# Experts of a mixture-of-experts stage taken in the order of their token counts, found on the chip

## The reference, cut to what matters

```
logits = xt @ w_router + b_router                      # 256 x 32
top_logits, top_idx = top_k(logits, 4); top_w = softmax(top_logits)
for each expert e, for its tokens:
    gate, up = split(xb @ w_gu[e] + b_gu[e], 2)
    act = (clip(up, -7, 7) + 1) * (min(gate, 7) * sigmoid(1.702 * gate))
    y[tok] += top_w * (act @ w_dn[e] + b_dn[e])
```

## Time and profile before

| | |
|---|---|
| median of 3 runs | 2322.34 us |
| lowest, highest | 2320.06, 2329.26 us |
| the profiled execution | 2318.49 us, span 2316.6 us |
| granted TensorE clock over the span | 0.983 |
| busy TensorE, VectorE, ScalarE | 2165.1, 751.5, 468.7 us |
| share of q1 (SyncE's transfers) of 16 DMA engines | 63.2% |
| transfers of w_gu, w_dn | 128 and 64, of 2048 KB |

### The profile page before, as it was taken

One profiled execution on the slowest core, in us unless ns is written; L12 is line 12 of the kernel. 1 busy time (PEld: TensorE's weight loads), 2 busy tenths in 40 slices (PEclk: granted clock), 3 DMA queues, 4 the chain that ended last, 5 costly groups with the idle time before them and its releaser, 6 DMA issues.

```text
span 2316.6 us, 30267 instructions
## 1 busy us (share of the span) xinstructions
PE 2165.1 (93%) x11523; PEld 1138.8 (49%) x11524; DVE 751.5 (32%) x1836; ACT 468.7 (20%) x930; POOL 65.4 (3%) x79
## 2 busy tenths in 40 slices
PE   5999998989999998999989998999999999999998
PEld 4844455343333333333333334844565446787873
DVE  1596234212222222222211223232212353988100
ACT  1011102111111111111110111131112215898100
POOL 0000000000000000000000000000000000222000
PEclk9999998999999999999999999999999999999999
DMA  9645557859999999999996799435133323232241
GB/s 345 223 163 181 209 196 285 337 224 417 418 418 418 418 418 381 418 417 418 417 383 265 317 417 384 148 112 200 68 141 133 123 103 125 74 110 74 103 164 42
DMA packets 158855, 591.31 MB, mean 255 GB/s; under 512 B 5323, under 2 KB 6927, under 8 KB 125887
## 3 DMA queue, kind: packets, MB, share of 16 engines
q1 hardware_dynamic: 152512, 573.08, 63.2%
q0 software_dynamic: 4384, 16.40, 2.0%
q10 hardware_dynamic: 1887, 0.81, 0.1%
HBM read 589.23 MB, written 1.05 MB: 255 GB/s over the span
## 4 chain that ended last, share of the span: by engine, by line
PE 74%; DMA 15%; DVE 5%; ACT 3%; DVEq 2%; issue 1%; ACTq 0%; SPq 0%
PE PS L616 22%; PE PS L922 13%; DMA W<-in_w_gu 13%; PE PS L604 10%; PE PS L945 6%; PE PS L1129 4%; PE PS L631 4%; PE PS L869 2%; PE PS L958 2%; PE PS L1202 1%; DVE BIG L1924 1%; PE PS L886 1%; DVE BIG L1928 1%; DMA W<-in_w_mod 1%; DVEq L1927 1%
## 5 line engine op out<-in xcount | busy, mean ns | idle before, releaser
L616 PE MATMUL PS<-W,BIG 128*128 128x512 f32 x1152 | 501.0, 596 | 5.0 <-DVE BIG L2358 2.9
L922 PE MATMUL PS<-W,BIG 128*64 128x512 f32 x2048 | 451.8, 595 | 21.0 <-DMA W<-in_w_gu 20.9
L616 PEld LDWEIGHTS PS<-W,BIG 128*128 128x128 f32 x1152 | 219.4, 191 | 277.2 <-issue 270.5
L922 PEld LDWEIGHTS PS<-W,BIG 128*64 128x64 f32 x2048 | 142.1, 137 | 313.0 <-issue 270.8
L945 PE MATMUL PS<-W,BIG 128*64 128x512 f32 x1024 | 228.8, 600 | 7.0 <-ACT BIG L1408 6.9
L604 PE MATMUL PS<-BIG,W 128*128 128x256 f32 x1024 | 222.2, 379 | 1.4 <-ACT BIG L354 1.4
L604 PEld LDWEIGHTS PS<-BIG,W 128*128 128x128 f32 x1024 | 194.2, 190 | 28.9 <-ACT BIG L354 1.9
L1922 DVE TENSOR_SCALAR BIG<-PS 128x512 f32<-128x512 f32 (+1 forms) x38 | 24.7, 650 | 379.6 <-PE PS L922 355.9
L945 PEld LDWEIGHTS PS<-W,BIG 128*64 128x64 f32 x1024 | 71.1, 138 | 144.0 <-issue 126.3
L1403 ACT ACTIVATE BIG<-BIG 128x512 f32<-128x512 f32 x32 | 20.2, 632 | 488.9 <-DVE BIG L1922 488.9
L1129 PE MATMUL PS<-BIG,W 128*128 128x256 f32 x512 | 118.3, 385 | 0.5 <-ACT BIG L1563 0.5
(11 more groups left out here) (460 smaller groups left out, 1963.2 us busy)
## 6 DMA issues: line engine op xcount, KB each, us to landing
W<-in_w_gu SPq DMA_DIRECT2D x128, 2048.0 KB, 17.3
W<-in_w_dn SPq DMA_DIRECT2D x64, 2048.0 KB, 19.1
W<-in_w_in SPq DMA_DIRECT2D x24, 2048.0 KB, 15.1
W<-in_w_mod SPq DMA_DIRECT2D x12, 2048.0 KB, 9.6
W<-in_gla_w_in SPq DMA_DIRECT2D x10, 2048.0 KB, 7.9
W<-in_s_w_in SPq DMA_DIRECT2D x8, 2048.0 KB, 8.9
W<-in_s_w_glu SPq DMA_DIRECT2D x8, 2048.0 KB, 8.0
W<-in_w_out SPq DMA_DIRECT2D x6, 2048.0 KB, 8.3
```

Of the source, the lines that this page charges most:

```text
L616: ins = pe.matmul(ps[:, t, :], lhs(i * KT + k)[:, t * P:(t + 1) * P], w[:, k, :], start=i + k == 0, stop=last_chunk and k == KT - 1)
L922: ins = pe.matmul(PS[hh[h], g, :], XET[:, k, :], gu_w(k)[:, g * D + h * CH:g * D + (h + 1) * CH], start=False, stop=k == KT - 1, skip_grou ...
```

## The change

A table PERM gives the expert that stands at each place. It is worked out on the chip: each expert's key is its token count times 32 minus its number, and expert 0 has a key above all others. The rank of an expert is the number of keys above its own. So expert 0 comes first, the others follow from the heaviest to the lightest. TensorE counts each expert's tokens once more in a column (OWN_COUNT), VectorE compares and ranks (seven instructions), and two small products bring counts and numbers into the order of places. The table of extra blocks is then made from the counts in that order. C_PLACE is the identity here.

SyncE reads the expert's number from PERM for each place but the first. VectorE reads it at the head of each expert (for the next one) and once more within each heavy expert. TensorE and ScalarE go by places as before.

```
@@ load_expert (SyncE) @@
-                        gu = A["w_gu"][0, bass.ds(e, 1)].rearrange("e (k p) n -> p (e k) n", p=P)
-                        dn = A["w_dn"][0, bass.ds(e, 1)].rearrange("e (k p) n -> p (e k) n", p=P)
+                        source = e if previous is None else sp.value_load(PERM[0:1, bass.ds(e, 1)], min_val=0, max_val=NE - 1)
+                        gu = A["w_gu"][0, bass.ds(source, 1)].rearrange("e (k p) n -> p (e k) n", p=P)
+                        dn = A["w_dn"][0, bass.ds(source, 1)].rearrange("e (k p) n -> p (e k) n", p=P)
@@ TensorE, ahead of pos_done @@
+            for t in range(TT):
+                pe.matmul(OWN_COUNT, SEL[:, t, :], ONES[:, 0:1], start=t == 0, stop=t == TT - 1)
@@ TensorE, behind the first gather @@
             gather_rows(0, True)
+            pe.wait_ge(ev("sel_ready"), 2)
+            pe.matmul(PLACED_COUNT, RANK[:, 0:1], ORDER, start=True, stop=True)
+            pe.matmul(PLACED_EXPERT, K[0:NE, C_OWN + 1:C_OWN + 2], ORDER, start=True, stop=True).then_inc(ev("pos_done"), 1)
@@ VectorE, extras and expert @@
+            def placed(e):
+                return dve.value_load(PERM[0:1, bass.ds(e, 1)], min_val=0, max_val=NE - 1)
                 with dve.If(hi - lo > 0):
+                    own = placed(e)
                     with dve.Fori(lo, hi) as x:
-                        extra_block(x, e, nc.s_assert_within(x - lo + 1, 1, XMAX))
+                        extra_block(x, own, nc.s_assert_within(x - lo + 1, 1, XMAX))
                 if not last:
-                    one_hot(e + 1, K[:, C_SLOT:C_SLOT + BLK], PW, G, GW, ev("g_ready"))
+                    following = placed(e + 1)
+                    one_hot(following, K[:, C_SLOT:C_SLOT + BLK], PW, G, GW, ev("g_ready"))
@@ VectorE, ahead of the table @@
-            cnt, nx = pos[0:1, 2, :], TABF[:, 0, :]
+            dve.tensor_copy(RANK[:, 0:1], OWN_COUNT)
+            dve.scalar_tensor_tensor(KEY, pos[0:NE, 2, :], float(NE), K[0:NE, C_TIE:C_TIE + NE], ALU.mult, ALU.add)
+            dve.scalar_tensor_tensor(RANK[:, 1:2], OWN_COUNT, float(NE), K[0:NE, C_OWN:C_OWN + 1], ALU.mult, ALU.add)
+            dve.drain()
+            dve.tensor_scalar(ABOVE, KEY, RANK[:, 1:2], None, ALU.is_gt)
+            dve.drain()
+            dve.tensor_tensor_scan(KEY, ONES[0:NE, 0:NE], ABOVE, 0.0, ALU.mult, ALU.add)
+            dve.drain()
+            dve.tensor_scalar(ORDER, K[0:NE, C_PLACE:C_PLACE + NE], KEY[:, NE - 1:NE], None, ALU.is_equal)
+            dve.drain()
+            dve.sem_inc(ev("sel_ready"), 1)
+            dve.wait_ge(ev("pos_done"), 2)
+            dve.tensor_copy(PERM, PLACED_EXPERT)
+            cnt, nx = PLACED_COUNT, TABF[:, 0, :]
```

More of the change, by code:

```diff
@@ L51 @@
 C_N = C_T + T
+C_TIE = C_SLOT + P + (XMAX + 1) * XBLK
+C_PLACE = C_TIE + NE
+C_OWN = C_PLACE + NE
 R_C, R_AV, R_AG, R_CB, R_BS = 0, 8, 16, 24, 32
@@ L67, in constants @@
     c[:, C_T:C_T + T] = np.arange(T)
+    own = -np.arange(NE, dtype=np.float32)
+    own[0] = 4 * T * NE
+    c[:, C_TIE:C_TIE + NE] = own
+    c[0:NE, C_OWN] = own
+    c[0:NE, C_OWN + 1] = np.arange(NE)
+    spread = list(range(NE))
+    c[:, C_PLACE + np.array(spread)] = np.arange(NE)
     half = P // 2
@@ L356, in copy_columns @@
                                ACT.Copy).then_inc(tp_copied, 1)
+        PERM = BIG[0:1, 7 * ROW + D + 968:7 * ROW + D + 968 + NE].bitcast(I32)
         TABX = MISC[0:1, 2 * P:2 * P + 6 * NE].rearrange("p (j e) -> p j e", j=6).bitcast(I32)
@@ L463, in build @@
         TABI = BIG[0:1, E7 + 896:E7 + 896 + 2 * NE].rearrange("p (a e) -> p a e", a=2).bitcast(I32)
+        RANK = BIG[0:NE, E7 + 1000:E7 + 1002]
+        KEY, ABOVE, ORDER = OH[0:NE, 0, :], OH[0:NE, 1, :], LG[0:NE, 0, :]
+        OWN_COUNT, PLACED_COUNT, PLACED_EXPERT = PS[0:NE, 2, 0:1], PS[0:1, 2, NE:2 * NE], PS[0:1, 2, 2 * NE:3 * NE]
         WMT = BIG[0:NE, 8 * ROW:8 * ROW + T].rearrange("p (t s) -> p t s", t=TT)
@@ L1905, in one_hot_extra, with columns_of @@
                         K[:, C_SLOT + P + j * XBLK:C_SLOT + P + (j + 1) * XBLK], PWX, GX, GWX, ev("x_g_ready"))
-            def columns_of(e):
-                dve.tensor_copy(SELB[0:NE], ident[0:NE, bass.ds(e, 1)].to_broadcast([NE, BLK]))
-                dve.tensor_copy(SELB[NE:2 * NE], ident[NE:2 * NE, bass.ds(e + NE, 1)].to_broadcast([NE, BLK])) \
+            def columns_of(e, own):
+                dve.tensor_copy(SELB[0:NE], ident[0:NE, bass.ds(own, 1)].to_broadcast([NE, BLK]))
+                dve.tensor_copy(SELB[NE:2 * NE], ident[NE:2 * NE, bass.ds(own + NE, 1)].to_broadcast([NE, BLK])) \
                     .then_inc(ev("selb_ready"), 1)
@@ L1954, in expert @@
                 if not last:
-                    columns_of(e + 1)
-                    one_hot_extra(e + 1, 0)
+                    columns_of(e + 1, following)
+                    one_hot_extra(following, 0)
                 dve.drain()
@@ L1977, in _ @@
             dve.sem_inc(ev("table_ready"), 1)
-            columns_of(0)
+            columns_of(0, 0)
             one_hot_extra(0, 0)
```

## The result

| | before | changed |
|---|---|---|
| median | 2320.3 us (5 runs, 2318.3 to 2329.3) | 2343.6 us (5 runs, 2342.0 to 2349.1) |
| ratio | | 1.0096, 95% interval 1.0077 to 1.0114 |
| the profiled execution, its span | 2318.5, 2316.6 us | 2342.1, 2340.3 us |
| granted TensorE clock over the span | 0.983 | 0.983 |

What follows compares the result with a forecast made beforehand. Light experts were taken as bound by weight transfers (30.12 us against TensorE's 27.79) once the 13.6 us stock is used. Terms 20.6 + 2.5 + 1.0 = 24.1 us gave a median of 2346 us, range 2337 to 2358.

Steps and rivals of the forecast that it cites:

- The order: Expert stage: five heavy experts in a row fill the stock once, starvation rises from 26.3 to 46.95 us, +20.6 us.
- the stock: Expert stage: transfers' lead over TensorE, 13.6 us, filled by one extra block; each free light expert uses 2.33.
- The loads: Added expert-number loads: only VectorE's within each of five heavy experts lies open, 0.5 each, +2.5 us; SyncE's hidden.
- The start: Before the first expert: added small products and ranking delay the table, mostly covered by waits, +1.0 us.
- the covered case: Before the first expert: most of the table's 3.2 us delay hides behind existing waits, 0.8 to 1.0 remains.
- The clock: Heavy experts' blocks: granted clock falls in two of six again, +0; all six would be +6 us.
- A growing stock: Rival, expert stage: five heavy experts in a row fill all 30.1 us of the ring, 2330 us; 5 in 100.
- An unchanged order: Rival, ranking: order comes out as identity or loads read the old number, 2326 us; 2 in 100.
- Faster transfers in another order: Rival, expert stage: transfers take under 30.12 us an expert; starvation falls below 26.3 under 29.2 us; 2 in 100.
- The clock falling more often: Rival, expert stage: half the starved experts and all blocks pay a 1.45 us clock fall, 2366 us; 5 in 100.
- The sum: Whole kernel: order 20.6, loads 2.5 and start 1.0 make 24.1 us more, median 2346 us; 86 in 100.

Runs made afterwards that it cites:

- the pairs: Changed kernel with heavy experts at places 1, 2, 13, 14 and 25 instead of 1 to 5: 2324.1 us, ratio 1.0014 to the kernel before.
- the half transfers: Changed kernel with half of each gate/up transfer left out inside the expert loop: 2294.4 us, ratio 0.9892 to the kernel before.
- the undone and the spread orders: Changed kernel with keys giving order 0 to 31 again: 2326.1 us; changed kernel with heavy experts at places 5, 11, 17, 23, 28: 2299.0 us.
- The late refill: Changed kernel with each slot in the loop refilled only once the chunk behind it was used too: 2348.4 us, ratio 1.0112 to the kernel before.

## Why the prediction was right, point by point

**The order, +20.6.** Measured 21.2 in the profiles. The pattern (five free, a sixth of 28.1, then 30.12) came as read from the earlier trace rows; the 0.6 more lie in the last place. There its wait for bytes cost the 2.3 of any starved expert, the pause ahead of the turned activation was 3.91 us instead of 3.09, and the down product, at the lower clock in part in both kernels, took 8.95 instead of 9.14. Why the pause was longer is open: VectorE's last step ended 1.8 us before TensorE went on, against 1.0 before, and the pause was 3.89 in the pairs too, where the last place did not starve. That the stock is capped by one heavy expert was read from two places of the trace before; the pairs show it, within 1 us. That bytes alone make the starved period is shown by the half transfers, that the order makes it by the undone and the spread orders.

**The size of the stock** was read from the trace as 13.6 us, with no account of why it is less than half of the 30.1 that the ring holds. The late refill shows what it hangs on: when the moment at which the transfers get going again in an expert came 4.9 us later, the stock was 5.0 smaller. The expectation of that run took the delay to be one chunk of 3.49; the 13.6 itself is not derived by it.

**The loads, +2.5.** Measured 3.6. The step was right (VectorE is the late one there, all of the load lies open), its size 0.71 to 0.77 instead of 0.5. It came from "two loads and a branch take 1.47"; half of that would have been the better value: with the third load the same pause is 2.24, so a load is 0.77, and nothing is left of the 1.47 for the branch. The Trainium skill, in "DMA: Bandwidth & Descriptors", "Latency and other measured facts", has a floor of some 600 ns for a tensor_load; the 0.71 to 0.77 measured here with two register instructions agree with it, and by an estimate it would have given 3.0 for the five, where 3.6 were measured. SyncE's load is hidden, as forecast, but it isn't free: its pause with seven loads is 5.2 us (674.4 to 679.6 above), and 4.5 with six in the kernel before. It stays without effect: in the changed kernel the transfers moved 418 GB/s on the mean from 660 to 740 us, across three such pauses.

**The start, +1.0.** From the first product of the counts to the first gate product of expert 0:

```profile
372.07 0.41 PE L814 MATMUL PS<-BIG,K 128*128 128x32 f32 x2 [0.46 <-DVEq L1898]
...
378.29 0.21 PE L985 MATMUL PS<-BIG 32*1 32x32 f32 x2
...
378.60 0.18 DVE L2000 CAST BIG<-PS 1x32 int32<-1x32 f32 x1 [1.23 <-PE PS L986]
...
381.50 0.18 DVE L1928 COPY BIG<-K 32x64 f32<-32x64 f32 x1 [0.21 <-issue]
...
385.16 5.37 PE L939 MATMUL PS<-W,BIG 128*64 128x512 f32 x24
```

That is 13.09 us; in the profile before the same stretch ran from 373.90 (L799) to 386.36, 12.46. So 0.6, the covered case. VectorE waits 1.23 for TensorE's gather, as said, and the table, ready near 381.3, is in time. The stage as a whole began 1.2 us earlier than before, though, and between the profiled executions of all kernels here its beginning lies anywhere from 383.9 to 391.1 with nearly the same instructions ahead. The clock has a part in it: the last two records of 512 columns ahead of expert 0 (L826) took 1.02 us in the changed kernel and 1.89 with the order undone, and the first six 2.74, but 4.44 in the changed kernel run again. A difference of 1 us at the start can't be read from the beginning of the stage.

**The clock, 0.** It fell twice for 1.44 in the profile after, as before. The table above says that this was luck: the same kernel, run again, lost 7.6 us to it, and one heavy expert with one block took 51.65 there. The prediction priced a fall at 1.45 and had +6 as its upper end, for a fall in every block; falls of some 4.6 came too, and the pairs stood 10.9 above the 2.9. The changed kernel was profiled twice, with spans of 2340.3 and 2348.4; 4.7 of these 8.1 us are the clock in its heavy experts.

**The rivals.** A growing stock: the pairs leave 0.7 to 1.0 for the second heavy expert instead of 16. An unchanged order: 2326 was its price, and the kernel in which the order is undone took 2326.1; that the two agree so well is luck, since the price was 3.5 us on a median of 2322 and the run showed 6.6 on one of 2319.6. Faster transfers in another order: the starved period was 30.12 in every order in which light experts starved, and the slices stand at 417 to 418. The clock falling more often: none of the 19 starved experts in the loop showed a fall (all took 30.11 to 30.14), and the heavy ones had two, as before.

**The sum.** 24.1 us were forecast for the profiled execution and 23.7 measured. Some of that closeness is luck: the order and the loads were forecast 1.7 us too low, and the beginning of the stage came 1.2 earlier where 1.0 later was forecast. That the median is 2343.6 and not 2346 is mostly the kernel before: 2322.3 was the median of three runs, 2320.3 is that of five.

## What to carry to other kernels

When a loop alternates between a limit by compute and a limit by transfers, the order of its items decides how much of the surplus of one kind can be kept for the other, and the buffer caps it: here 13.6 us, filled by a single heavy item. Read the cap from the trace (how many items run free behind a heavy one) and place a heavy item wherever it runs out; the orders with all heavy items in a row, first or last, were the slowest of those tried. A term that comes from a wait of two engines should be taken with all that stands in the pause, and a gain of 3 us can't be told in the time of a few runs where falls of the clock of 1.3 to 4.8 us come and go.

## What the runs showed of the hardware that was not expected

The granted clock fell in some executions of the same block and not in others: an expert of the same instructions took 47.03, 48.4 or 51.6 us, and 64.55, 66.2 or, with the starved part, 71.4. What went ahead was alike each time, TensorE waiting some 1.24 and then 0.6 to 1.3 us between short products. Within the profile of the changed kernel, place 2 waited 1.25 and 1.32 us and did its first product of the extra block in 7.11; place 3 waited 1.25 and 1.29 and took 8.57. What decides between the two is not shown.

The end of a loop is worth a look of its own: without the gather of a next item to fill the pause, the last light expert ran its down product in 8.95 us instead of 7.09 (8.4 to 10.1 in the other kernels that end with a light one), and in the four kernels with a heavy one in its place it took 7.09.
